# Stick-breaking attention: values projected by token, their differences taken between rows; late last input tiles

## The reference, cut to what matters

```
qkv = (hn @ w_qkv).reshape(b, s, 3, SB_HEADS, HEAD_DIM)
z = einsum('bqhd,bshd->bhqs', q, k) * scale
log_1m = where(causal, log_sigmoid(-z), 0.0)
excl = cumsum(log_1m, axis=3, reverse=True) - log_1m
a = where(causal, exp(log_sigmoid(z) + excl), 0.0)
o = einsum('bhqs,bshd->bqhd', a, v);  h = h + o @ w_o
```

## Time and profile before

| | |
|---|---|
| median of 3 runs | 2010.76 us (2008.69 to 2012.25) |
| profiled execution | 2009.92 us, its span 2008.1 us |
| TensorE busy | 1956.7 us, 97% of the span |
| VectorE, ScalarE, GpSimd busy | 68%, 45%, 12% |
| granted clock, mean | 0.994 |

### The profile page before, as it was taken

One profiled execution on the slowest core, in us unless ns is written; L12 is line 12 of the kernel. 1 busy time (PEld: TensorE's weight loads), 2 busy tenths in 40 slices (PEclk: granted clock), 3 DMA queues, 4 the chain that ended last, 5 costly groups with the idle time before them and its releaser, 6 DMA issues.

```text
span 2008.1 us, 28428 instructions
## 1 busy us (share of the span) xinstructions
PE 1956.7 (97%) x11514; PEld 1653.9 (82%) x11514; DVE 1366.2 (68%) x1904; ACT 894.9 (45%) x1362; POOL 247.5 (12%) x315
## 2 busy tenths in 40 slices
PE   9999999999999999999999999998899999999998
PEld 7877789999888777778899898886688778899896
DVE  5347587776774668857777776778674357776774
ACT  4227443343442777645343434666552334433432
POOL 1010000000003226520000000074400300000001
PEclk9999999999999999999999999999999999999998
DMA  5320123223234430012223233221134123233231
GB/s 198 105 84 1 63 87 104 103 90 121 84 106 147 147 106 2 2 43 87 102 86 122 87 105 105 90 85 52 43 122 151 42 84 105 84 106 105 85 119 49
DMA packets 29867, 181.28 MB, mean 90 GB/s; under 512 B 4720, under 2 KB 5744, under 8 KB 9264
## 3 DMA queue, kind: packets, MB, share of 16 engines
q1 hardware_dynamic: 26928, 172.16, 25.0%
q0 software_dynamic: 1952, 6.03, 1.1%
q10 hardware_dynamic: 864, 1.36, 0.2%
HBM read 172.72 MB, written 2.10 MB: 87 GB/s over the span
## 4 chain that ended last, share of the span: by engine, by line
PE 88%; DVE 6%; ACT 3%; issue 2%; POOL 1%; DMA 0%; POOLq 0%; ACTq 0%; DVEq 0%
PE ps L569 26%; PE ps L570 25%; PE ps L571 25%; PE ps L1840 2%; PE ps L1801 2%; PE ps L1820 2%; PE ps L1142 1%; PE ps L1127 1%; DVE w_lo L555 1%; ACT leftT L1193 1%; DVE f_probs L1622 1%; PE ps L1290 1%; PE ps L1268 1%; ACT turned_keys L2043 0%; DVE x_res L494 0%
## 5 line engine op out<-in xcount | busy, mean ns | idle before, releaser
L569 PE MATMUL ps<-o_hi,w_hi 128*128 128x512 f32 x1024 | 400.7, 391 | 6.8 <-DVE o_lo L1372 2.5
L570 PE MATMUL ps<-o_lo,w_hi 128*128 128x512 f32 x1024 | 398.9, 390 | 0.0
L571 PE MATMUL ps<-o_hi,w_lo 128*128 128x512 f32 x1024 | 398.5, 389 | 0.0
L569 PE MATMUL ps<-h_hi,w_hi 128*128 128x512 f32 (+1 forms) x960 | 344.2, 359 | 7.2 <-DVE w_lo L548 3.6
L538 ACT ACTIVATE w_hi<-w_raw 128x2048 fp32r<-128x2048 f32 x109 | 208.6, 1914 | 301.2 <-PE ps L571 296.0
L570 PE MATMUL ps<-h_lo,w_hi 128*128 128x512 f32 (+1 forms) x960 | 341.3, 355 | 0.0
L571 PE MATMUL ps<-h_hi,w_lo 128*128 128x512 f32 (+1 forms) x960 | 341.2, 355 | 0.0
L555 DVE TENSOR_TENSOR w_lo<-w_raw,w_hi 128x2048 fp32r<-128x2048 f32 x109 | 252.8, 2319 | 62.8 <-ACT w_hi L538 62.7
L569 PEld LDWEIGHTS ps<-o_hi,w_hi 128*128 128x128 f32 x1024 | 192.4, 188 | 47.7 <-DVE o_lo L1372 3.3
L571 PEld LDWEIGHTS ps<-o_hi,w_lo 128*128 128x128 f32 x1024 | 192.2, 188 | 40.4
L570 PEld LDWEIGHTS ps<-o_lo,w_hi 128*128 128x128 f32 x1024 | 192.4, 188 | 38.2 <-issue 0.2
(11 more groups left out here) (355 smaller groups left out, 3482.8 us busy)
## 6 DMA issues: line engine op xcount, KB each, us to landing
w_raw<-in_wstream SPq DMA_DIRECT2D x159, 1024.0 KB, 4.9
x_res<-in_xT SPq DMA_DIRECT2D x4, 512.0 KB, 5.0
e_cmp<-kv_nat POOLq DMA_DIRECT2D x8, 128.0 KB, 6.4
k_slc<-kv_nat POOLq DMA_DIRECT2D x8, 128.0 KB, 2.7
k_win<-kv_nat POOLq DMA_DIRECT2D x8, 128.0 KB, 10.3
mem_in<-in_memT POOLq DMA_DIRECT2D x1, 1024.0 KB, 5.3
out_T<-x_res SPq DMA_DIRECT2D x4, 256.0 KB, 2.2
out_T<-x_res ACTq DMA_DIRECT2D x4, 256.0 KB, 2.9
```

The lines of the kernel that those rows point to most:

```text
L569: pe.matmul(o, l_hi, r_hi, start=first, stop=False)
L570: pe.matmul(o, l_hi, r_lo, start=False, stop=False)
L571: return pe.matmul(o, l_lo, r_hi, start=False, stop=last)
```

## The change

Four edits. First, blocks 8 to 11 are laid out by `wide_blocks` and run by `tensor_wide`, so that v comes out with tokens in the partitions (`v_sb`); VectorE empties two banks with one instruction and scales by `rcol`, a factor by partition, which the first norm must now make as well ("TN"). Second, the differences lie between partitions: for each half of the columns GpSimd issues two transfers inside the on-chip memory, which move all rows down by one (127 partitions of 4 times 2 KB, and the seams between the four tiles), waits for both, and subtracts; the value turns and their copies are gone. Third, EARLY is 3: scores of units 0, 1 and 2 stand in the middle of blocks 8, 9 and 10. Fourth, in the first block of `sb_o`, `nsa_o`, `out` and `co` the passes of the last input tile (of two in `co`) come after the other passes of both output tiles.

```diff
-            mix0=norm(None, [x_split(g_of("mix0"))], [(x, S, None, acc)], "T"),
+            mix0=norm(None, [x_split(g_of("mix0"))], [(x, S, None, acc)], "TN"),
...
+            behind = order[KT - late:]
...
+                    if k in behind:
+                        continue
...
+            for j in tiles if late else ():
+                for k in behind:
+                    if j == 0:
+                        wait(pe, *(ready(k) if callable(ready) else (ready[0], ready[1] + ready[2] * k + 1)))
...
+                if free_at is not None:
+                    pe.wait_ge(tile_free, free_at + t // 2)
...
-        EARLY = 2
+        EARLY = 3
...
-                if k // 2 + 1 < PAIRS:
-                    for i in (0, 1):
-                        mm = turn_values(k // 2 + 1, 2 * (k % 2) + i, 4 * S + 10 * P + P * i)
...
+                pe.wait_ge(k_step, p // 4 + 1)
...
-            for p in range(PAIRS):
-                pool.wait_ge(tile_free, 4 + 2 * (b["sb_qkv"] + 8) + p + 1)
-                step, v = sb_qk[:, 2 * PAIRS + p, :], v_tile[:, p % 2, :]
-                pool.tensor_scalar(step[:, 0:1], v[:, 0:1], -1.0, None, ALU.mult)
-                pool.tensor_tensor(step[:, 1:S], v[:, 0:S - 1], v[:, 1:S], ALU.subtract).then_inc(k_v, 1)
+            pool.memset(shifted_rows[0:1, :, 0, :], 0.0).then_inc(k_zero, 1)
+            for c in (0, 1):
+                rows = v_sb[:, :, S * c:S * c + S]
+                pool.wait_ge(tile_free, 4 + 2 * (b["sb_qkv"] + 10 + 2 * c))
+                pool.dma_start(shifted_rows[1:P, c, :, :], rows[0:P - 1, :, :]).then_inc(k_shift, 16)
+                pool.dma_start(shifted_rows[0:1, c, 1:QT, :], rows[P - 1:P, 0:QT - 1, :]).then_inc(k_shift, 16)
+                pool.wait_ge(k_shift, 32 * (c + 1))
+                pool.wait_ge(k_zero, 1)
+                pool.tensor_tensor(rows, shifted_rows[:, c, :, :], rows, ALU.subtract).then_inc(k_step, 1)
...
+            for q in range(4):
+                blk = b["sb_qkv"] + 8 + q
...
+                tensor_wide(pe, blk, q % 2, h_hi, h_lo, (0, 1, 2, 3), inner=early if q < EARLY else None,
+                            free_at=4 + 2 * blk - 1 if q == 2 else None)
...
-            tensor_linear_T(pe, b["sb_o"], 4, o_hi, o_lo, ready=(k_lo, 0, 1), last=last)
+            tensor_linear_T(pe, b["sb_o"], 4, o_hi, o_lo, ready=(k_lo, 0, 1), last=last, late=1)
...
-            tensor_linear_T(pe, b["co"], 4, o_hi, o_lo, ready=lambda k: (c_olo, k // 2 + 1), last=last)
+            tensor_linear_T(pe, b["co"], 4, o_hi, o_lo, ready=lambda k: (c_olo, k // 2 + 1), last=last, late=2)
...
+                if q % 2 == 0:
+                    dve.engine_nop().then_inc(tile_free, 2)
+                if q < EARLY:
+                    scan(q)
+                for j in (0, 1) if q % 2 else ():
                     dve.wait_ge(tile_done, 2 * blk + j + 1)
-                    value_tile(q // 2, q % 2, j, 2 * (blk % 2) + j).then_inc(tile_free, 1)
+                    dve.tensor_tensor(v_sb[:, 2 * j:2 * j + 2, S * (q // 2):S * (q // 2) + S], ps[:, 2 * j:2 * j + 2, :],
+                                      rcol[:, 2 * j:2 * j + 2].unsqueeze(2).broadcast_to([P, 2, S]), ALU.mult).then_inc(tile_free, 1)
```

More of the change, by code:

```diff
@@ L224, in build_program @@
         late_done, late_free = sem("late_done"), sem("late_free")
-        k_mask, k_s, k_left, k_scan, k_v, k_first, k_begun, k_t, k_c, k_steps, k_pv, k_hi, k_lo = (sem("k_" + n) for n in (
-            "mask", "s", "left", "scan", "v", "first", "begun", "t", "c", "steps", "pv", "hi", "lo"))
+        k_mask, k_s, k_left, k_scan, k_zero, k_shift, k_step, k_t, k_c, k_pv, k_hi, k_lo = (sem("k_" + n) for n in (
+            "mask", "s", "left", "scan", "zero", "shift", "step", "t", "c", "pv", "hi", "lo"))
         c_s, c_mx, c_nm, c_p, c_rc, c_pn, c_t, c_c0, c_c1, c_pv, c_ohi, c_olo = (sem("x_" + n) for n in (
@@ L654, in tensor_block_N, with tensor_wide @@
                 mm.then_inc(tile_done, 1)
-        def tensor_wide(pe, blk, half, a_hi, a_lo, banks, inner=None):
+        def tensor_wide(pe, blk, half, a_hi, a_lo, banks, inner=None, free_at=None):
             par = blk % 2
@@ L667, in tensor_wide @@
                     inner()
-                if half == 0 and bank < 4:
+                if free_at is not None:
+                    pe.wait_ge(tile_free, free_at + t // 2)
+                elif half == 0 and bank < 4:
                     pe.wait_ge(tile_free, 2 * blk + t + 1)
@@ L690, in run_between, with tensor_linear_T @@
                 between[2 * i + u](eng)
-        def tensor_linear_T(pe, first, n, r_hi, r_lo, tokens=S, ready=None, root=None, between=None, order=tuple(range(KT)), last=None):
+        def tensor_linear_T(pe, first, n, r_hi, r_lo, tokens=S, ready=None, root=None, between=None, order=tuple(range(KT)), last=None, late=0):
             def step(i, u):
@@ L697, in step @@
                 tensor_block_T(pe, first + 2 * i + u, (first + u) % 2, r_hi, r_lo, tokens, ready if head else None,
-                               root=root if rooted else None, order=order, last=last if head else None)
+                               root=root if rooted else None, order=order, last=last if head else None, late=late if head else 0)
                 run_between(pe, between, i, u)
@@ L1177, in second @@
                 turn(STEPS - 1)
-            return first_values, first_scores, lambda pe: scores(1), rest, {3: second, 7: lambda: values(STEPS - 1)}
+            return scores, rest, {3: second, 7: lambda: values(STEPS - 1)}
         def scalar_sb(act):
@@ L1208, in high @@
                     act.activation(o_hi[:, k // 2, :], ps[:, 7, :], ACT.Copy).then_inc(k_hi, 1)
-            def early(act):
-                for k in range(EARLY):
-                    beta(k)
             def rest():
+                copy(0)
                 for m in range(EARLY, STEPS + 3):
@@ L1217, in rest @@
                         beta(m)
-                    if m >= 3:
-                        high(m - 3)
-                    if 2 <= m < STEPS + 2:
+                    high(m - 3)
+                    if m < STEPS + 2:
                         copy(m - 2)
-            return copy_first, early, rest
+            return beta, rest
         def vector_sb(dve):
@@ L1237, in rest @@
                 for m in range(EARLY, STEPS + 3):
-                    if m >= 3:
-                        low(m - 3)
+                    low(m - 3)
                     if m < STEPS:
@@ L2372, in _, with early @@
             tensor_linear_T(pe, b["sb_qkv"] + 1, 7, h_hi, h_lo, root="mix0")
[L2373 to L2377, removed]
+            for q in range(4):
+                blk = b["sb_qkv"] + 8 + q
+                def early(k=q):
+                    if k == 0:
+                        pe.wait_ge(tile_free, 4 + 2 * (b["sb_qkv"] + 8))
+                    stick_scores(k)
+                tensor_wide(pe, blk, q % 2, h_hi, h_lo, (0, 1, 2, 3), inner=early if q < EARLY else None,
+                            free_at=4 + 2 * blk - 1 if q == 2 else None)
             stick_rest()
-            tensor_linear_T(pe, b["sb_o"], 4, o_hi, o_lo, ready=(k_lo, 0, 1), last=last)
+            tensor_linear_T(pe, b["sb_o"], 4, o_hi, o_lo, ready=(k_lo, 0, 1), last=last, late=1)
             tensor_mlp(pe, 0, "mlp0")
@@ L2402, in _ @@
             sparse_rest()
-            tensor_linear_T(pe, b["nsa_o"], 4, o_hi, o_lo, ready=(n_olo, 0, 1), last=last)
+            tensor_linear_T(pe, b["nsa_o"], 4, o_hi, o_lo, ready=(n_olo, 0, 1), last=last, late=1)
             tensor_mlp(pe, 1, "mlp1")
```

73 lines of the change are left out of this document (21 added, 52 removed).

## The result

The changed kernel took 2063.41 us (2062.44 to 2064.71), the kernel before 2010.47 us on the same chip: ratio 1.0261, 95% interval 1.0247 to 1.0275, 53 us slower. The profiled execution took 2062.44 us, its span 2060.6 us, mean granted clock 0.978 (0.994 before). Lines of the changed kernel stand a little lower: the values' passes are L1144, their turns L1132, the transfers L1230 and L1231, GpSimd's subtraction L1234.

What follows compares the result with a forecast made beforehand. TensorE, busy 97% of the span, was taken as the bound. Terms 3.5 + 0.5 - 1.0 + 5.3 + 0.6 = 8.9 us off took the median from 2010.76 to 2001.8 us; range 1999.5 to 2004.5, or 1997.5 to 2009 with all rivals but (a).

Steps and rivals of the forecast that it cites:

- The moved rows: Attention stage: GpSimd's row transfers and subtractions finish before the values need them; cost 0, loss at most 5.3 us.
- Rival (a): Attention stage: the 127-row transfer runs on one of 16 DMA engines, TensorE stands 52 us, 2054 us in all; chance 10%.
- The value turns: Attention stage: removing the value turns shortens the unit period from 4.10 to 3.88 us; 3.5 us gained.
- the third early unit: Scores of unit 2 moved into block 10, ahead of the attention units; 0.5 us gained.
- the projection by token: Blocks 8 to 11: weights and tokens exchange roles, with 48 passes each of the same length; cost 0.
- VectorE in time for block 10: Block 10: VectorE empties banks 0 and 1 after scan 1 before TensorE arrives, hidden with 0.5 us to spare.
- The first norm: Before block 2: "TN" adds steps to the chain that block 2 waits for; 1.0 us lost, between 0.8 and 1.4.
- The dip of the clock: TensorE at half speed after a wait, 1.4 us each; one or two more or fewer, 2.8 us either way, in no term.
- GpSimd against VectorE: Attention stage: GpSimd's second subtraction holding VectorE off its scans; taken as 0, loss at most 5.3 us.
- Late tiles: First blocks of `sb_o`, `nsa_o`, `co`: passes moved before the `o_lo` wait gain 1.4, 1.4 and 2.5 us, 5.3 together.
- rival (d): Late tiles do nothing, as the first output tile's release in `co` or `nsa_o` becomes the wait; 2007 us; chance 4%.
- At `out`: Late tile in `out`: 0.6 us gained, bounds 0 and 1.4, the rest returning as a longer wait in `ckv`.

Runs made afterwards that it cites:

- experiment 9: experiment 8 with VectorE instead of GpSimd subtracting the moved rows; 1997.85 us, ratio 0.9939 to the kernel before.
- experiment 11: experiment 9 with two early units in place of three (`EARLY = 2`); 1999.95 us, ratio 0.9945 to the kernel before.
- experiment 1: The changed kernel with each 127-row transfer issued as two, of 112 and 15 rows; 2001.87 us, ratio 0.9951 to the kernel before.
- experiment 2: The changed kernel with each 127-row transfer issued as two, of 124 and 3 rows; 2012.58 us in one execution.
- experiment 3: The changed kernel with all 128 rows transferred unshifted, without seams and zeroed first row; 1999.39 us in one execution.
- experiment 6: experiment 1 without the late input tiles in all four calls; 2009.9 us, ratio 0.9996 to the kernel before.
- experiment 7: `before_tn`: the kernel before with only the first norm changed to kind "TN"; 2013.04 us, ratio 1.0008 to the kernel before.
- experiment 4: The changed kernel with its 127-row transfers and 3-row seams issued from ScalarE's queue instead of GpSimd's; 2059.69 us in one execution.
- experiment 8: experiment 1 with the first norm's factor by partition made after the one for rows; 1998.36 us, ratio 0.9941 to the kernel before.
- experiment 10: experiment 9 without the late input tile in `out`; 1999.4 us, ratio 0.9939 to the kernel before.
- experiment 5: The kernel before with the late input tiles alone (`sb_o`, `nsa_o`, `out`, `co`); 2000.61 us, ratio 0.9947 to the kernel before.

## Why the prediction was wrong

**The step that failed is "The moved rows", "Cost 0".** It cost 63.5 us: 37.0 and 21.8 of stalls and 4.7 of passes at half speed behind them. I had priced the transfer from rows with 64 and 128 partitions, 5.3 and 10.3 us, and bounded it by those. They were no neighbours in the one property that counted, the divisibility of the leading size. The rest of that step held: block 9 was freed at 128.5 us (forecast 128), the subtraction took 4.5 us (4.2 to 9.4), and unit 8 wanted the second half 33.5 us after values 0 began, 8 x 3.88 = 31.0 and 2.5 of half speed.

**Rival (a) is what happened**, at 10%. The mechanism is shown: 127 rows at a DMA share of 0.06 to 0.07 from either queue, 124 rows at 0.25, 112 + 15 and 128 rows in 5 to 6 us, with 1, 4 and 16 packets at once. By the Trainium skill (DMA: Bandwidth & Descriptors, section "Why a DMA increments its semaphore by 16 and not by 1") the number of engines is the largest up to 16 that divides the leading size, 1 for 127, 4 for 124 and 16 for 112 and 128. The traces agree on all four; the page's exception, some direct copies from GpSimd's queue on all 16, did not apply to this transfer. The rival's sum gave 2054 us and not 2063 because two things were missing. The first half was ready at 190.07 and not 182: the issue was taken at 1 us and was 4.8, and 51.4 us of waiting followed where the sum had 49. That the 49 came so near is partly luck: one engine moved 25 to 26 GB/s, not the sum's 21, so 1.04 MB alone would have taken 41 us; but by 150 us, 16 us behind the issue, only 0.25 MB had moved, in 3907 packets of which nearly all were under 512 bytes. And the passes behind each stall ran at half speed, 4.7 us.

I set the transfers of 64 partitions "on the same queue" against the rival. That was no evidence: 64 has 16 as a divisor, so by this rule they would have spread in any case. For an event that costs 52 us or more and that no row excludes, 10% was too low, and a range that ended at 2009 left it out.

**The value turns and the third early unit**: right. Period 3.88 us as worked out, 4.05 us together (forecast 4.0), and 4.1 in experiment 9's distance from block 2 to `sb_o`. That leaves nothing for the projection by token either, as forecast. By experiment 11 the shares are 0.85 and 3.2 in place of 0.5 and 3.5.

**VectorE in time for block 10**: right, no wait there.

**The first norm**: right on the chain (0.97 us, forecast 1.0). The dip of the clock behind it, which I had left outside the sum at 1.4 us, occurred in experiments 1, 2, 3, 6 and 7 and cost 1.5 to 1.6 us; it did not occur in the changed kernel itself, nor in experiment 4.

**GpSimd against VectorE**: wrong in its mechanism, small in its size. I took 0 "since no row shows a VectorE instruction stopped by GpSimd for its whole length". Once the transfer is fast, one is stopped for 4.3 us, and TensorE loses 1.4 (experiment 9 against 8) of the bound of 5.3. In the changed kernel nothing of this shows, as the scans were over when GpSimd subtracted. The Trainium skill (SBUF — State Buffer, section "Who interferes with whom") says that a VectorE instruction with two inputs in SBUF and a GpSimd one that reads SBUF exclude each other for a whole instruction; experiments 1 and 3 agree, with sums of whole durations on both sides.

**Late tiles**: right at `sb_o`, `nsa_o` and `co`, 1.50, 1.48 and 2.78 us for 1.4, 1.4 and 2.5, and rival (d) is excluded: the release of the first output tile became no wait. At `out` 1.15 us stand for 0.6, but experiments 9 and 10 set a loss of 0.75 against it, so the sign of that one is open. In experiment 5 the late tiles alone bring the whole gain that can be measured.

**The forecast without the failed step.** Experiment 1 is the change as I had pictured it, 2001.87 us against 2001.8. That the two agree is partly luck: the late tiles gave 1 us more than forecast, while GpSimd's hold on VectorE and the clock behind block 2 took 3 us that no term held. The rest was evened out in part by other stretches of the clock: the trace of experiment 1 did not meet the one at 673 us (1.6 us), had less of one at the last norm (1.0) and met one more in `ckv` (1.5). The forecast had put such stretches at up to 2.8 us either way.

**Open**: why a wait of 2.39 us before block 2 was followed by a half-speed stretch in `before_tn` and not in the changed kernel, nor, after 2.45 us, in experiment 4. Open too: why GpSimd's queue took 4112 packets for a half of 127 rows and 320 for 112 + 15.

## What to carry to other kernels

Before a transfer is put on the path, look at the leading size of both its sides: for 127 rows, two transfers of 112 and 15 took one issue more, 0.6 us, and saved 61 us. A price by the nearest row is only as good as the property in which the two are near; ask which property of a transfer the known rows all share (here a leading size that 16 divides), and treat the first one without it as unpriced. And test the parts of a bundle by themselves: of the four edits the late tiles carried the measured gain and the moved rows the whole loss, and with the rows spread the other three together came to nothing until the norm's columns had left the chain.

## What the runs showed of the hardware

- A transfer of 127 rows of 8 KB within SBUF ran at 25 to 26 GB/s on one DMA engine (share 0.06 to 0.07) from GpSimd's queue and from ScalarE's alike; 124 rows ran at 83 GB/s on four (0.25), and 112 + 15 rows landed in 5.9 us. From GpSimd's queue the issue itself grew, 4.8 us for 127 rows, 1.8 for 124, 0.95 for 112.
- From ScalarE's queue the next transfer could not be issued for 34 to 37 us while the slow one ran, and the engine's own instructions stood behind it.
- Scans of VectorE and a subtraction of GpSimd, both with two inputs in SBUF, took turns in experiments 1 and 3: 5.53 + 4.5 us took 9.8 and 9.9 us together, whichever began.
- After 37 and 22 us of standing still TensorE ran 1.3 us groups in 2.4 us, at 1.2 GHz, which cost 2.3 us a stall. After a wait of 2.39 us before block 2 the clock was lowered for 3.4 us in `before_tn` and not in the changed kernel.
